# Gate, up and MLP-up products: from one 512-wide and one 256-wide product per weight block to three 256-wide ones, with the activations at the shifted place

## The chip, the cores and the metric

The kernel runs on one core of one Trainium2 chip. The metric is the device time of one execution in microseconds (us). TensorE (PE) multiplies into PSUM, VectorE (DVE) and ScalarE (ACT) read PSUM and SBUF, GpSimd (POOL) does a few small things, SyncE (SP) issues the weight transfers.

## The reference

Two model blocks run one after the other on 256 tokens of width 1024, all in float32. The first block has two layers (a multiscale pooling mixer, then a differential attention), each followed by a layernorm and a SwiGLU feed-forward part (FFN) of width 2816 with its own layernorm. The second block has a token mixer with many projections, and an MLP of width 4096 with a squared relu:

```python
def _swiglu(x, w_gate, w_up, w_down):
    return (jax.nn.silu(x @ w_gate) * (x @ w_up)) @ w_down

for i in range(DEPTH):                       # 2 layers
    h = pool or attention (x)
    x = _layernorm(ALPHA * x + h, ln_mix_g[i], ln_mix_b[i])
    x = _layernorm(ALPHA * x + _swiglu(x, w_gate[i], w_up[i], w_down[i]), ln_ffn_g[i], ln_ffn_b[i])

x = x + token_mixer(rms_norm(x, norm_mix_g), w_in, ...)
x = x + jnp.square(jax.nn.relu(rms_norm(x, norm_mlp_g) @ w_up)) @ w_down
return rms_norm(x, final_norm_g)
```

The change touches `x @ w_gate`, `x @ w_up` of the two FFNs and `x @ w_up` of the MLP.

## The kernel before, in words

**Precision in three products.** Every float32 operand of a large product is split into a rounded part and its remainder (`w_hi` and `w_lo` for weights, `x_hi` and `x_lo` for activations, type fp32r), and a product is the sum w_hi·x_hi + w_hi·x_lo + w_lo·x_hi in PSUM.

**Units.** Weights stream through three slots. A unit is 1 MB of weights, 2048 numbers in each of the 128 partitions. SP loads it into `raw` by two transfers of 512 KB (each waits until `lo_done` says that the slot is free), ACT rounds it into `w_hi` (two instructions, L1043), DVE takes the remainder into `w_lo` (two instructions, L1055, signalled by `lo_done`), and PE uses it (`unit_done` counts the units that PE has finished). A gate or up unit holds 1024 rows by 256 columns of weights: eight blocks k of 128 rows, two blocks j of 128 columns. All matrix products are recorded at line L505 (`mm`), so the operand names tell them apart: `bank<-x_both,w_hi` has weights stationary and activations moving, `bank<-w_hi,arena_r` is the down product, with the hidden values stationary and the down weights moving, 512 columns at a time.

**Gate and up before.** `apart` uses that x_hi and x_lo lie beside each other in `x_both`: for a block (j, k) one product of w_hi with 512 moving columns gives both halves, and one of w_lo with the 256 columns of x_hi adds to the first half. The two column blocks j of a unit take two whole PSUM banks (gate 4 and 5, up 6 and 7), and DVE adds the halves afterwards (`both_halves`, a tensor_reduce at L1515). `project_apart` runs all w_hi products of a unit and then all w_lo products, or the other way round (`narrow_first`, for up). A unit is thus 16 products of 512 and 16 of 256 columns.

**Three products elsewhere.** The attention heads and the projections of the token mixer use `project`, which makes for each block three products of 256 columns into half a bank (`three`): w_hi·x_hi, w_hi·x_lo, w_lo·x_hi. The last up of each FFN and of the MLP uses it too (`final=True`), so DVE adds nothing there.

**Two places for x_both.** `x_cells` has 48 spare numbers. `x_both` starts at its beginning (the near place), `x_far` 48 numbers (192 bytes) later (the far place: `far_hi`, `far_lo`). `normed` says where a norm writes: far for the norms ahead of the attention (V_NORM) and ahead of the token mixer (MIX_NORM), near for the norms ahead of both FFNs and of the MLP. The final ups mentioned above thus run `project` on the near place, the heads and the mixer on the far one.

**An FFN chunk.** The FFN goes through 11 chunks of 256 hidden columns (`NCH`), each a gate unit, an up unit and the down unit of the chunk before. PE waits with a gate for `gate_read` (DVE has read banks 4 and 5 of the chunk before) and with an up for `up_read`. DVE's order in a chunk is: remainder of one unit, `gate_total` (adds the gate's halves), remainder of the next unit, `silu`, `hidden` (adds the up's halves and multiplies), remainder, `low`. ACT takes the tanh of the added gate from SBUF (L1105) and rounds the hidden values (L1112). The MLP (`pe_mlp`, `v_mlp`, `s_mlp`) has 16 chunks of an up and a down unit; there DVE adds the halves and squares.

**The first units of a stage.** `first_apart` starts on the first four k as soon as their activations are ready. In the first FFN the order on DVE is: remainders of units 0, 1 and 2 (six instructions), `gate_total(0)`, remainder of unit 3, `silu(0)`, `hidden(0)`. Unit 3 (the second up) can be loaded only when unit 0's slot is free. The third unit on PE is the gate of chunk 1.

## Time and profile before

| | |
|---|---|
| median of 3 runs | 964.71 us (963.29 to 966.46) |
| the profiled execution | 966.28 us, of which 964.5 us are its span |
| PE busy | 951.7 us, 99% of the span, 5903 matmuls |
| PE weight loads (beside the matmuls) | 840.5 us, 87% |
| DVE busy | 674.4 us, 70% |
| ACT busy | 468.5 us, 49% |
| TensorE clock granted, mean | 0.997 |

A matmul's duration in the records (some 280 ns for 256 columns, 390 ns for 512) contains the way through the array and overlaps with the next one. What a stream of matmuls costs is the distance from one start to the next, read from the timeline: start of a row to the start of a later one, divided by the number of matmuls between. In the timeline each row is: start in us, length in us, engine, line, operation, result and operands, shape, number of instructions merged, and in brackets the idle time before it and what ended it. A few matmul records are missing from the trace, so counts are taken from the code where the timeline shows fewer.

### The profile page before, as it was taken

Reading aid. Unit: us, or ns where it says so; the run is one execution under the profiler, and the core shown is the slowest. Engines: PE = TensorE matmul, PEld = TensorE weight load, DVE = VectorE, ACT = ScalarE, POOL = GpSimd, SP = SyncE. Lnnn points to the kernel's source line nnn. Section 1 sums busy time; section 2 is a strip of 40 time slices with the busy share of each in tenths; the row PEclk is TensorE's granted clock in tenths of the full one; section 3 lists DMA queues with packets and bytes.
Section 4 is the critical chain, followed back from the end, with each engine's and each line's share of the span. In section 5 each row is a group of like instructions: output and inputs, shape, how many; then the busy total and the mean of one; then the engine's idle time right before and its main releaser. Section 6 shows DMA issues by size and latency. Waiting matters only on the chain.

```text
span 964.5 us, 15378 instructions
## 1 busy us (share of the span) xinstructions
PE 951.7 (99%) x5903; PEld 840.5 (87%) x5903; DVE 674.4 (70%) x968; ACT 468.5 (49%) x721; POOL 34.6 (4%) x63
## 2 busy tenths in 40 slices
PE   9999999999999999999999999999999999999997
PEld 8888888887898888888898989899999888888886
DVE  2877676776687886767768577886876676666663
ACT  3454344335766443434435556566654453443432
POOL 2100001000000100000001000000000000000000
PEclk9999999999999999999999999999999999999999
DMA  8666666548632566565653855445566546565541
GB/s 296 203 214 220 204 207 238 187 174 226 168 132 89 170 221 206 202 206 175 214 175 125 238 157 144 138 132 154 175 209 201 182 137 211 185 206 178 202 145 43
DMA packets 142160, 175.67 MB, mean 182 GB/s; under 512 B 7152, under 2 KB 121009, under 8 KB 142110
## 3 DMA queue, kind: packets, MB, share of 16 engines
q1 hardware_dynamic: 138896, 166.55, 53.9%
q0 software_dynamic: 2656, 8.31, 2.6%
q8 instruction: 34, 0.56, 0.2%
q10 hardware_dynamic: 558, 0.12, 0.1%
q14 instruction: 16, 0.13, 0.0%
HBM read 173.88 MB, written 1.09 MB: 181 GB/s over the span
## 4 chain that ended last, share of the span: by engine, by line
PE 93%; DVE 4%; ACT 2%; issue 1%; POOL 0%; DVEq 0%; POOLq 0%
PE bank L505 91%; PE bank L752 1%; DVE x_both L1443 1%; PE bank L629 1%; DVE w_lo L1055 0%; DVE x_rows L1471 0%; DVE x_rows L1464 0%; DVE stats L1456 0%; ACT w_hi L1043 0%; ACT x_both L1082 0%; ACT arena L1331 0%; PE bank L641 0%; ACT arena L1168 0%; DVE arena L1645 0%; ACT arena L1307 0%
## 5 line engine op out<-in xcount | busy, mean ns | idle before, releaser
L505 PE MATMUL bank<-x_both,w_hi 128*128 128x256 f32 (+1 forms) x2112 | 428.1, 328 | 0.5 <-DVE x_both L1443 0.5
L1055 DVE TENSOR_TENSOR w_lo<-raw,w_hi 128x1024 fp32r<-128x1024 f32 x308 | 362.6, 1221 | 92.3 <-ACT w_hi L1043 92.1
L505 PEld LDWEIGHTS bank<-x_both,w_hi 128*128 128x128 f32 x2112 | 351.5, 188 | 40.9 <-issue 6.5
L1043 ACT ACTIVATE w_hi<-raw 128x1024 fp32r<-128x1024 f32 x308 | 308.0, 1049 | 99.3 <-PE bank L505 95.0
L505 PE MATMUL bank<-x_both,w_lo 128*128 128x256 f32 (+1 forms) x1512 | 282.6, 281 | 0.0
L505 PEld LDWEIGHTS bank<-x_both,w_lo 128*128 128x128 f32 (+1 forms) x1512 | 227.3, 190 | 3.0
L505 PE MATMUL bank<-w_hi,arena_r 128*128 128x512 f32 x672 | 189.6, 391 | 0.2 <-DVE arena_r L1592 0.2
L505 PEld LDWEIGHTS bank<-w_hi,arena_r 128*128 128x128 f32 x672 | 124.8, 188 | 25.7 <-issue 0.8
L505 PE MATMUL bank<-w_lo,arena_r 128*128 128x512 f32 x336 | 106.3, 390 | 0.0
L1515 DVE TENSOR_REDUCE arena<-bank 128x512 f32<-128x1024 f32 x57 | 69.7, 1223 | 47.9 <-PE bank L505 47.9
L505 PEld LDWEIGHTS bank<-w_lo,arena_r 128*128 128x128 f32 x336 | 63.1, 188 | 13.2
L1105 ACT ACTIVATE arena<-arena 128x512 f32<-128x512 f32 x22 | 13.9, 632 | 92.9 <-DVE arena L1515 92.9
L505 PE MATMUL bank<-arena 128*128 128x128 f32 (+5 forms) x368 | 54.3, 350 | 3.2 <-ACT arena L1203 2.1
L505 PE MATMUL bank<-w_hi,x_both 128*128 128x512 f32 x192 | 55.9, 395 | 1.0 <-DVE x_both L1443 1.0
L505 PEld LDWEIGHTS bank<-arena 64*128 64x128 f32 (+2 forms) x368 | 38.4, 190 | 13.3 <-issue 6.8
L1112 ACT ACTIVATE arena_r<-arena 128x512 fp32r<-128x512 f32 x22 | 13.9, 634 | 70.1 <-PE bank L505 60.5
L505 PEld LDWEIGHTS bank<-w_hi,x_both 128*128 128x128 f32 x192 | 35.8, 188 | 10.1 <-issue 1.8
L1203 ACT ACTIVATE arena<-bank 128x512 f32<-128x512 f32 x22 | 13.1, 597 | 49.8 <-PE bank L505 49.8
L1548 DVE TENSOR_TENSOR arena_r<-arena,arena_r 128x512 fp32r<-128x512 f32 x22 | 15.2, 692 | 31.4 <-ACT arena_r L1112 31.4
L1139 ACT ACTIVATE arena_r<-arena 128x512 fp32r<-128x512 f32 x16 | 10.1, 634 | 55.1 <-PE bank L505 48.1
L505 PE MATMUL bank<-arena_r,w_hi 128*128 128x256 f32 x192 | 32.9, 276 | 0.0
L505 PE MATMUL bank<-w_lo,x_both 128*128 128x512 f32 x96 | 31.9, 392 | 0.0
(168 smaller groups left out, 600.9 us busy)
## 6 DMA issues: line engine op xcount, KB each, us to landing
raw<-w_up SPq DMA_DIRECT2D x76, 512.0 KB, 4.5
raw<-w_down SPq DMA_DIRECT2D x76, 512.0 KB, 4.1
raw<-w_in SPq DMA_DIRECT2D x60, 512.0 KB, 4.6
raw<-w_gate SPq DMA_DIRECT2D x44, 512.0 KB, 4.7
raw<-w_qkv SPq DMA_DIRECT2D x24, 512.0 KB, 4.8
raw<-w_o SPq DMA_DIRECT2D x16, 512.0 KB, 4.0
table<-bias_vectors POOLq DMA_DIRECT2D x12, 256.0 KB, 4.2
raw<-w_pa SPq DMA_DIRECT2D x4, 512.0 KB, 4.4
```

Of the source, the lines that this page charges most:

```text
L505: return nc.tensor.matmul(*a, skip_group_check=True, **k)
L629: last = nc.tensor.transpose(b[:, k * P:(k + 1) * P], src[:, i, (4 * h + k) * P:(4 * h + k + 1) * P], ident[:, :])
L752: last = nc.tensor.transpose(bank[6 + m][:, c], prob[:, m, c], ident[:, :])
L1043: nc.scalar.activation(w_hi[slot][:, c], raw[slot][:, c], ACT.Copy).then_inc(hi_done, 1)
L1055: last = nc.vector.tensor_tensor(w_lo[slot][:, c], raw[slot][:, c], w_hi[slot][:, c].bitcast(F32), ALU.subtract)
L1105: nc.scalar.activation(ffn_e.rearrange("p (a b) -> p a b", a=2), gate_sum, ACT.Tanh, scale=0.5).then_inc(tanh_done, 1)
L1112: nc.scalar.activation(h_hi[buf], hidden_rows, ACT.Copy).then_inc(h_rounded, 1)
L1139: nc.scalar.activation(h_hi[buf], hidden_rows, ACT.Copy).then_inc(m_rounded, 1)
L1203: nc.scalar.activation(dst, both, ACT.Copy).then_inc(proj_copied, 1)
L1443: V.tensor_tensor(lo[:, k, q], src, hi[:, k, q].bitcast(F32), ALU.subtract).then_inc(x_ready, 1)
L1515: return V.tensor_reduce(o, banks8[:, b:b + 2, :].rearrange("p a (h t) -> p a t h", h=2), mybir.AxisListType.X, ALU.add)
L1548: V.tensor_tensor(h_lo[buf], ffn_h.rearrange("p (a b) -> p a b", a=2), h_hi[buf].bitcast(F32), ALU.subtract).then_inc(h_ready, 1)
```

## The change

The two FFNs and the MLP use `project` for all gates and ups, so each unit is 48 products of 256 columns instead of 16 of 512 and 16 of 256. A new `first_project` does the same for the first units: per half of k all w_hi products, first x_hi and then x_lo, and at the end the w_lo products. A unit's result is one bank (gate 4, up 6; MLP 4, its second chunk 6). `both_halves` and its semaphores go. `tanh_of` and the relu (now on ACT for all chunks) read the bank itself; `silu`, `hidden` and `square` on DVE take one operand from the bank. `gate_read`, for which PE waits with the next gate, is now signalled by `silu`, and PE waits with the next up for `product_done` in place of `up_read`. All norms write x_both at the far place.

```diff
-        def apart(banks, w, cols, ks, first):
-            for j, b in enumerate(banks):
-                for k in ks:
-                    last = mm(b[:, 0:cols], w[:, k, j * P:(j + 1) * P], x_both[:, k, 0:cols],
-                              start=(first and k == 0), stop=(not first and k == KT - 1))
-            return last
...
-        def first_apart(eng, unit, rounds, banks):
+        def first_project(eng, unit, rounds, outs):
             whi, wlo = (part(w, unit % SLOTS, KT) for w in (w_hi, w_lo))
             eng.wait_ge(hi_done, 2 * unit + 2)
             for h in range(2):
                 eng.wait_ge(x_ready, 4 * rounds + 2 * h + 2)
-                apart(banks, whi, 2 * SEQ, range(4 * h, 4 * h + 4), True)
+                for j, o in enumerate(outs):
+                    for k in range(4 * h, 4 * h + 4):
+                        for src in (far_hi, far_lo):
+                            mm(o, whi[:, k, j * P:(j + 1) * P], src[:, k, :],
+                               start=(j == 0 and k == 0 and src is far_hi), stop=False)
             eng.wait_ge(lo_done, unit + 1)
-            return apart(banks, wlo, SEQ, range(KT), False)
+            for j, o in enumerate(outs):
+                for k in range(KT):
+                    last = mm(o, wlo[:, k, j * P:(j + 1) * P], far_hi[:, k, :], start=False, stop=(k == KT - 1))
+            return last
...
         def normed(ev):
-            return (far_hi, far_lo) if ev in (V_NORM, MIX_NORM) else (x_hi, x_lo)
+            return far_hi, far_lo
...
-            def gate_up(i, unit, final=False):
+            def gate_up(i, unit):
                 eng.wait_ge(lo_done, unit + 1)
                 eng.wait_ge(gate_read, i + f * NCH)
-                project_apart(slots[0], pair45).then_inc(unit_done, 1)
+                project(slots[0], two4, far_hi, far_lo).then_inc(unit_done, 1)
                 eng.wait_ge(lo_done, unit + 2)
-                eng.wait_ge(up_read, i + f * NCH)
-                if final:
-                    project(slots[1], two6, x_hi, x_lo).then_inc(unit_done, 1)
-                else:
-                    project_apart(slots[1], pair67, True).then_inc(unit_done, 1)
+                eng.wait_ge(product_done, i + f * NCH)
+                project(slots[1], two6, far_hi, far_lo).then_inc(unit_done, 1)
...
-            first_apart(eng, u0, rounds, pair45).then_inc(unit_done, 1)
-            eng.wait_ge(hi_done, 2 * u0 + 4)
-            project_apart((u0 + 1) % SLOTS, pair67, False,
-                          lambda: eng.wait_ge(lo_done, u0 + 2)).then_inc(unit_done, 1)
+            first_project(eng, u0, rounds, two4).then_inc(unit_done, 1)
+            first_project(eng, u0 + 1, rounds, two6).then_inc(unit_done, 1)
             gate_up(1, u0 + 2)
...
         def s_ffn(eng, f):
-            def tanh_of(i):
-                eng.wait_ge(gate_read, i + (f * NCH + 1))
-                nc.scalar.activation(ffn_e.rearrange("p (a b) -> p a b", a=2), gate_sum, ACT.Tanh,
-                                     scale=0.5).then_inc(tanh_done, 1)
+            def tanh_of(i, gate_unit, begin=False):
+                eng.wait_ge(unit_done, gate_unit + 1)
+                if not begin:
+                    eng.wait_ge(gate_read, i + f * NCH)
+                nc.scalar.activation(ffn_e, bank[4][:, :], ACT.Tanh, scale=0.5).then_inc(tanh_done, 1)
...
+            def relu(i, unit, b=4, begin=False):
+                eng.wait_ge(unit_done, unit + 1)
+                if not begin:
+                    eng.wait_ge(sq_done, i)
+                nc.scalar.activation(ffn_e, bank[b][:, :], ACT.Relu).then_inc(relu_done, 1)
...
-        def both_halves(o, b):
-            return V.tensor_reduce(o, banks8[:, b:b + 2, :].rearrange("p a (h t) -> p a t h", h=2),
-                                   mybir.AxisListType.X, ALU.add)
...
             def silu(i):
                 eng.wait_ge(tanh_done, i + (f * NCH + 1))
-                V.scalar_tensor_tensor(ffn_t, ffn_e, 1.0, gate_sum.rearrange("p a b -> p (a b)"), ALU.add,
-                                       ALU.mult).then_inc(silu_done, 1)
+                V.scalar_tensor_tensor(ffn_t, ffn_e, 1.0, bank[4][:, :], ALU.add, ALU.mult).then_inc(gate_read, 1)
...
             v_split(eng, u0 + 2)
-            gate_total(0, u0)
             v_split(eng, u0 + 3)
             silu(0)
             hidden(0, u0 + 1)
```

PE at the start of an FFN, from its first product to the gate of chunk 1, before (the wait for `gate_read` is that of the third unit):

```order
L505 MATMUL bank<-x_both,w_hi 128x512 [waits x_ready,hi_done]
L505 MATMUL bank<-x_both,w_hi 128x512 x7
L505 MATMUL bank<-x_both,w_hi 128x512 [waits x_ready]
L505 MATMUL bank<-x_both,w_hi 128x512 x7
L505 MATMUL bank<-x_both,w_lo 128x256 [waits lo_done]
L505 MATMUL bank<-x_both,w_lo 128x256 x15
L505 MATMUL bank<-x_both,w_hi 128x512 [waits hi_done]
L505 MATMUL bank<-x_both,w_hi 128x512 x15
L505 MATMUL bank<-x_both,w_lo 128x256 [waits lo_done]
L505 MATMUL bank<-x_both,w_lo 128x256 x15
L505 MATMUL bank<-x_both,w_hi 128x512 [waits gate_read,lo_done]
L505 MATMUL bank<-x_both,w_hi 128x512 x15
```

and now, from the second unit on (mm is now at L501):

```order
L501 MATMUL bank<-x_both,w_hi 128x256 [waits x_ready,hi_done]
L501 MATMUL bank<-x_both,w_hi 128x256 x15
L501 MATMUL bank<-x_both,w_hi 128x256 [waits x_ready]
L501 MATMUL bank<-x_both,w_hi 128x256 x15
L501 MATMUL bank<-x_both,w_lo 128x256 [waits lo_done]
L501 MATMUL bank<-x_both,w_lo 128x256 x15
L501 MATMUL bank<-x_both,w_hi 128x256 [waits gate_read,lo_done]
L501 MATMUL bank<-x_both,w_hi 128x256
L501 MATMUL bank<-x_both,w_lo 128x256
L501 MATMUL bank<-x_both,w_hi 128x256 x2
```

The 512-wide products became pairs of 256-wide ones; the gate of chunk 1 still waits for `gate_read`. DVE at the same place, before (the first row holds the remainders of units 0, 1 and 2, L1515 adds the halves and signals `gate_read` at its first row here):

```order
L1055 TENSOR_TENSOR w_lo<-raw,w_hi 128x1024 [waits hi_done] x6
L1515 TENSOR_REDUCE arena<-bank 128x512 [waits unit_done]
L1055 TENSOR_TENSOR w_lo<-raw,w_hi 128x1024 [waits hi_done] x2
L1529 SCALAR_TENSOR_TENSOR arena<-arena 128x512 [waits tanh_done]
L1515 TENSOR_REDUCE arena<-bank 128x512 [waits unit_done]
L1540 SCALAR_TENSOR_TENSOR arena<-arena 128x512 [waits silu_done,up_read]
L1548 TENSOR_TENSOR arena_r<-arena,arena_r 128x512 [waits h_rounded]
```

and now (L1507 is `silu`, which signals `gate_read`; L1512 is `hidden`):

```order
L1030 TENSOR_TENSOR w_lo<-raw,w_hi 128x1024 [waits hi_done] x8
L1507 SCALAR_TENSOR_TENSOR arena<-arena,bank 128x512 [waits tanh_done]
L1512 SCALAR_TENSOR_TENSOR arena<-arena,bank 128x512 [waits gate_read,unit_done]
L1516 TENSOR_TENSOR arena_r<-arena,arena_r 128x512 [waits h_rounded]
L1524 UNCONDITIONAL_BRANCH
```

`gate_read` moved from an instruction that stood ahead of the remainder of unit 3 to one that stands behind it.

## Rows read from the trace of the kernel before

**Rows 1.** The page: busy time of each engine, and the shares of the chain.
```profile
PE 951.7 (99%) x5903; PEld 840.5 (87%) x5903; DVE 674.4 (70%) x968; ACT 468.5 (49%) x721; POOL 34.6 (4%) x63
PE 93%; DVE 4%; ACT 2%; issue 1%; POOL 0%; DVEq 0%; POOLq 0%
```
**Rows 2.** Timeline of PE: one chunk of the first FFN.
```profile
60.21 3.79 PE L505 MATMUL bank<-x_both,w_hi 128*128 128x512 f32 x16
63.84 4.00 PE L505 MATMUL bank<-x_both,w_lo 128*128 128x256 f32 x32
67.67 3.82 PE L505 MATMUL bank<-x_both,w_hi 128*128 128x512 f32 x16
71.32 0.62 PE L505 MATMUL bank<-w_hi,arena_r 128*128 128x512 f32 x2
...
76.76 3.79 PE L505 MATMUL bank<-x_both,w_hi 128*128 128x512 f32 x16
```
**Rows 3.** Timeline of PE: one chunk of the MLP.
```profile
919.52 3.79 PE L505 MATMUL bank<-x_both,w_hi 128*128 128x512 f32 x16
923.15 2.08 PE L505 MATMUL bank<-x_both,w_lo 128*128 128x256 f32 x16
925.06 0.63 PE L505 MATMUL bank<-w_hi,arena_r 128*128 128x512 f32 x2
...
930.53 3.79 PE L505 MATMUL bank<-x_both,w_hi 128*128 128x512 f32 x16
```
**Rows 4.** Timeline of PE: token mixer's gates, 32 triples at the far place.
```profile
705.99 0.39 PE L505 MATMUL bank<-x_both,w_hi 128*128 128x256 f32 x2
...
716.53 0.39 PE L505 MATMUL bank<-x_both,w_hi 128*128 128x256 f32 x2
```
**Rows 5.** Timeline of PE: first projections of the mixer, 40 triples, far place.
```profile
534.12 0.40 PE L505 MATMUL bank<-x_both,w_hi 128*128 128x256 f32 x2
...
547.90 0.40 PE L505 MATMUL bank<-x_both,w_hi 128*72 128x256 f32 x2
```
**Rows 6.** Timeline of PE: the MLP's last up, 16 triples, near place.
```profile
941.53 0.40 PE L505 MATMUL bank<-x_both,w_hi 128*128 128x256 f32 x2
...
946.93 0.40 PE L505 MATMUL bank<-x_both,w_hi 128*128 128x256 f32 x2
```
**Rows 7.** Timeline of PE: start of the first FFN.
```profile
32.40 3.91 PE L505 MATMUL bank<-x_both,w_hi 128*128 128x512 f32 x16 [0.17 <-DVE x_both L1443]
...
38.06 3.82 PE L505 MATMUL bank<-x_both,w_hi 128*128 128x512 f32 x16
...
43.63 3.82 PE L505 MATMUL bank<-x_both,w_hi 128*128 128x512 f32 x16
```
**Rows 8.** Timeline of SP's queue: the issue of unit 3.
```profile
35.75 0.92 SPq L391 DMA_DIRECT2D raw<-w_up  x2
```
**Rows 9.** Timeline of ACT: start of the first FFN.
```profile
41.43 0.63 ACT L1105 ACTIVATE arena<-arena 128x512 f32<-128x512 f32 x1 [5.44 <-DVE arena L1515]
42.68 2.01 ACT L1043 ACTIVATE w_hi<-raw 128x1024 fp32r<-128x1024 f32 x2 [0.62 <-DMA raw<-w_up]
```
**Rows 10.** Timeline of DVE: start of the first FFN.
```profile
40.17 1.22 DVE L1515 TENSOR_REDUCE arena<-bank 128x512 f32<-128x1024 f32 x1
43.77 2.36 DVE L1055 TENSOR_TENSOR w_lo<-raw,w_hi 128x1024 fp32r<-128x1024 f32 x2 [2.38 <-ACT w_hi L1043]
46.05 0.68 DVE L1529 SCALAR_TENSOR_TENSOR arena<-arena 128x512 f32<-128x512 f32 x1
```
**Rows 11.** Timeline of DVE: a loop chunk, and the start of the second FFN.
```profile
82.50 1.23 DVE L1515 TENSOR_REDUCE arena<-bank 128x512 f32<-128x1024 f32 x1 [1.56 <-PE bank L505]
...
87.65 0.69 DVE L1529 SCALAR_TENSOR_TENSOR arena<-arena 128x512 f32<-128x512 f32 x1
...
340.28 1.23 DVE L1515 TENSOR_REDUCE arena<-bank 128x512 f32<-128x1024 f32 x1 [0.26 <-PE bank L505]
```
**Rows 12.** One line of the kernel: the reduce that the change removes.
```profile
L1515 DVE TENSOR_REDUCE arena<-bank x57: 1217/1224/1227, 40.2 to 936.3; 128x512 f32<-128x1024 f32 x57
```
**Rows 13.** Stretches: PE, PEld, DVE, ACT, POOL busy, granted clock, DMA share.
```profile
7.00:10.40 3.40, 3.40 (x15) 1.79 (x15) 0.97 (x2) 0.35 (x1) 0.18 (x1) 1.00 0.88 270
10.50:13.80 3.30, 3.30 (x17) 3.30 (x16) 2.76 (x3) 1.79 (x4) 0.00 (x0) 0.50 1.09 379
```

More of the change, by code:

```diff
@@ L1139, in round_h @@
                 nc.scalar.activation(h_hi[buf], hidden_rows, ACT.Copy).then_inc(m_rounded, 1)
+            def relu(i, unit, b=4, begin=False):
+                eng.wait_ge(unit_done, unit + 1)
+                if not begin:
+                    eng.wait_ge(sq_done, i)
+                nc.scalar.activation(ffn_e, bank[b][:, :], ACT.Relu).then_inc(relu_done, 1)
             s_split(eng, U_MLP + 2)
+            relu(0, U_MLP, begin=True)
             round_h(0, None)
-            with eng.Fori(0, (NCH2 - 1) // 3 - 1) as i:
+            for j in range(3):
+                unit = U_MLP + 1 + 2 * j
+                s_split(eng, unit + 2)
+                relu(j + 1, unit, 4 if j else 6)
+                s_split(eng, unit + 3)
+                round_h(j + 1, unit + 2)
+            with eng.Fori(1, (NCH2 - 1) // 3 - 1) as i:
                 for j in range(3):
@@ L1152, in s_mlp @@
                 s_split(eng, unit + 2)
-                if c == NCH2 - 1:
-                    eng.wait_ge(unit_done, unit + 1)
-                    nc.scalar.activation(ffn_e, bank[4][:, :], ACT.Relu).then_inc(relu_done, 1)
+                relu(c, unit)
                 s_split(eng, unit + 3)
@@ L1568, in v_ffn @@
             v_split(eng, unit + 2)
-            gate_total(NCH - 1, unit)
             v_split(eng, unit + 3)
             silu(NCH - 1)
-            hidden(NCH - 1, unit + 1, bank[6][:, :])
+            hidden(NCH - 1, unit + 1)
             low(NCH - 1, 1)
@@ L1595, in v_mlp @@
             v_split(eng, U_MLP + 2)
[L1596 removed]
+            square(0, True)
             low(0)
@@ L1600, in v_mlp @@
                 v_split(eng, unit + 2)
-                square(j + 1, unit, b=4 if j else 6)
+                square(j + 1, b=4 if j else 6)
                 v_split(eng, unit + 3)
```

75 lines of the change are left out of this document (18 added, 57 removed).

## The prediction

> **What bounds the kernel now.** I read the page first: PE is busy for 951.7 of 964.5 us, and 93% of the chain that ended last is PE [rows 1]. So only two things count: how far apart matmuls start, and where PE is made to wait. Next the timeline of PE, since a matmul's recorded length says nothing of the distance to the next. In a chunk of the first FFN [rows 2] the 16 wide products of the gate take 63.84 - 60.21 = 3.63 us, 227 ns each; the 32 narrow ones of gate and up 3.83 us, 120 ns each; the wide ones of up 3.65 us; the 24 of the down product 5.44 us. The chunk's period is 16.55 us, without a gap. A chunk of the MLP takes 11.01 us, of which the down product, entered straight from narrow products, is 5.47 [rows 3]. DVE is 70% busy and waits for PE, so that it loses 57 reduces of 1.22 us [rows 12], 70 us of work, gives nothing by itself.
>
> **What three narrow products cost.** A block needs the same 768 columns either way. The trace shows three prices for a triple of 256-column products:
> - at the near place 0.360 us (15 distances in 5.40 us [rows 6]), 120 ns each;
> - at the far place in the mixer's gates 0.340 us (31 distances in 10.54 us [rows 4]), 113.3 ns each;
> - at the far place in the mixer's first projections 0.353 us (39 distances in 13.78 us [rows 5]), 117.8 ns each.
>
> The block before costs 227 + 120 = 347 ns. So the same edit is a gain of 7 ns a block at the fast far pace, a loss of 6 at the slow far pace and of 13 at the near pace; a unit has 16 blocks. The far place alone does not make the pace fast: going through the timeline by triples, far streams keep one pace from their first few matmuls to their end, over unit boundaries too. Of 22 entries into such a stream between 240.77 and 656.81 us, 12 settle at the fast pace and 10 at the slow one; most of them follow small matmuls and a pause of the array.
>
> Which pace will the FFN have? Its gates are entered straight from 24 evenly spaced wide products of the down unit, with no pause. Evenly spaced wide products run at 113.3 ns per 256 columns, just the fast pace, so nothing has to settle; that speaks for it. The one far stream that follows wide products directly without small ones between, and is slow [rows 5], speaks against. I take the fast pace for the chunks, and half and half for the units entered after small matmuls or a pause.
>
> **The sum at the fast pace.**
> - A chunk of an FFN in the loop: 32 triples at 0.340 are 10.88 us, and the down product, now entered from narrow ones, 5.47 [rows 3]: 16.35 against 16.55, -0.20. There are nine per layer, 18: -3.6 us.
> - The last chunk of each layer: gate 5.55 to 5.44, and the last up, which ran at the near place, 5.76 to 5.44: -0.43, twice: -0.86. The MLP's last up likewise: -0.32.
> - 14 further MLP chunks: 5.44 + 5.47 = 10.91 against 11.01: -1.4.
> - The first two units of the second FFN and the first of the MLP: -0.3.
> Together -6.5 us.
>
> **The new wait.** The gate of chunk 1 writes bank 4, which `silu(0)` now reads, so it waits for `silu(0)`. In the first FFN that instruction stands behind the remainder of unit 3. SP issues unit 3 at 35.75 [rows 8], when unit 0's slot is free. ACT waits for the transfer and starts to round at 42.68; this wait of 0.62 us is ended by the DMA, and before it ACT did the tanh [rows 9]. DVE takes the remainder from 43.77 and starts `silu(0)` at 46.05 [rows 10]. The tanh will be earlier, since it needs no reduce, but it is not what comes last: the transfer is, and its issue hangs on unit 0's remainder, which doesn't move. With 0.68 for `silu` (one operand in PSUM instead of SBUF, which I take at the same price; the far bound is the 1.22 of the reduce) and 0.1 for the signal, PE starts that gate at 46.83 instead of 43.63 [rows 7]: +3.2 us. What the first two units gain or lose there is hidden in this wait and counts nothing. Queued behind the waiting matmul is everything on PE; nothing there was idle before, so the 3.2 us stay.
>
> Elsewhere the wait has cover. In a loop chunk the gate ends at 82.50 and `silu` starts at 87.65 [rows 11], earlier once the reduce is gone, while the next gate starts at 76.76 + 16.55 = 93.3 [rows 2]. The next up waits for `hidden`, which needs the up before and 0.7 us, against 11 us of other work. In the second FFN the first gate's end shows at 340.28 [rows 11]; tanh 0.6, the first half of rounding 1.05, two remainders 2.4 and `silu` 0.7 make 344.9 to 345.1, and PE wants the gate of chunk 1 at 334.43 + 11.0 = 345.4. That is a cover of 0.3 to 0.5 us; were the tanh or the transfer late by 1 us, it would cost 0.5. In the MLP relu and square (1.3 us) lie beside a down product of 5.4.
>
> **Units entered after a pause.** Chunk 1 of the first FFN (after the new wait), four units of the second FFN and the first two of the MLP are entered like the mixer's units. At the slow pace each costs 16 x 13.3 ns = 0.21 us more; eight units at half chance: +0.85.
>
> Sum: -6.5 + 3.2 + 0.85 = -2.5 us. The profiled execution took 966.28 us, its span 964.5 and 1.8 around it; the change would make it 963.8. The median shown lies 1.6 us below that execution, so the forecast for the median is 964.71 - 2.5 = 962.2 us.
>
> **What might add to it.** A pause can cost clock. Early in the trace PE ran at full clock on matmuls with a single row of weights, and in the stretch after it, 10.50 to 13.80, it was granted 0.50, 1.2 GHz instead of 2.4 [rows 13]. If the new wait has the same effect, 3.3 us at half the clock lose 1.65 us: 963.9. I leave that inside the likeliest case, as its upper part.
>
> **Rivals.**
> 1. *The slow far pace in the chunks.* 32 triples at 0.353 plus 5.47 are 16.78, +0.23 a chunk, 18 times 4.1; an MLP chunk 11.12, +0.11, 14 times 1.6; the first units +0.3, the last ones about 0 (+0.11 and -0.11 per layer, -0.11 in the MLP). With the wait: 5.9 + 3.2 = +9.1, 973.8 us. For it: 10 of 22 entries, and [rows 5]. It decides from a pace of some 116 ns per product, where the gain of the chunks is gone and the wait remains: slower.
> 2. *Chunks of both paces,* half each: (-6.5 + 5.9) / 2 + 3.2 = +2.9, 967.6 us. For it: the heads and mixer units change pace from one entry to the next. Against: all chunks have one and the same entry.
> 3. *A fixed cost per matmul,* so that 256 columns cost 120 wherever they read. Then a chunk takes 11.52 + 5.47 = 16.99, +0.44, 18 times 7.9; last chunks +0.4, the MLP 14 x 0.22 = 3.1, first units 0.6; with the wait +15.2, 979.9 us. For it: near narrow and wide products both lie 13 ns above 256 and 512 columns at 2.4 GHz. Against: [rows 4] run at 113.3 over units on end.
> 4. *The wait does not come,* because the second up's transfer lands earlier or its order gives way: -6.5 + 0.4 = 958.6 us. The waiting order is in the code and the landing in [rows 9], so little speaks for it.
>
> The Trainium skill ("TensorE: Matmul & The Clock Gate", Back-to-back issue gap) states a warm distance of N / 2.4 + 2.5 ns, a fixed cost for each matmul. By it a block would go from 325 to 328 ns, some 2.3 us over 57 units, and with the wait the time would be about 970. Its direction is that of rival 3. The rows disagree with its size: they show 227 where it gives 216, and 113 or 120 where it gives 109.
>
> **How the numbers follow.** Chances: the forecast 0.57 (with and without loss of clock, 960.5 to 964.5), rival 1 0.20, rival 2 0.12, rival 3 0.04, rival 4 0.05, anything else 0.02. A measurement of this kernel tells 0.3% (2.9 us) from no change, so faster means below 961.8 and slower above 967.6. The forecast lies just inside no change: I give 0.23 of its 0.57 to faster and 0.34 to the same; rival 2 lies across the upper bound. Faster: 0.23 + 0.05 + 0.02 = 0.30. Same: 0.34 + 0.03 = 0.37. Slower: 0.20 + 0.09 + 0.04 = 0.33. The range has to take in rival 2 and most of rival 1: 960.0 to 974.0; the forecast's own is 960.5 to 964.5.
>
> **What the changed kernel's profile would show.** The step on the wait: PE idle some 3.3 us before the third unit of the first FFN, ended by the DVE instruction of `silu`, which starts near 46.05; nothing of the kind in the second FFN. The step on the pace: an FFN chunk of 16.35 us and triples 0.340 us apart; 16.78 and 0.353 mean rival 1, 16.99 and 0.360 rival 3. The loss of clock: a stretch at 0.50 behind the wait. DVE busy falls by some 70 us, and that should show in nothing else. I am wrong if the chunks' pace is not the fast one, or if PE doesn't wait for `silu(0)`.

## The result, and the profile after

The changed kernel took 974.96 us (median of 4 runs, 973.04 to 980.05) beside 965.59 us for the kernel before: a ratio of 1.0108, 95% interval [1.0076, 1.014]. It is slower by 1.1%. The forecast was 962.2 us, with a range of 960.0 to 974.0. The pace of the chunks is that of the first rival, priced at 973.8 us; how near that sum lies is in part luck, as the part on the prediction shows.

The profiled execution took 973.04 us with a span of 971.2; before it was 964.5. The page after, its busy times and the chain [rows 1]:

```profile
PE 954.8 (98%) x6815; PEld 879.8 (91%) x6815; DVE 609.5 (63%) x911; ACT 475.1 (49%) x736; POOL 34.6 (4%) x63
PE 91%; DVE 5%; ACT 2%; issue 1%; DMA 1%; POOL 0%; DVEq 0%; POOLq 0%; SPq 0%
```

The removed reduces took 69.7 us [rows 12]; DVE's busy time fell by 64.9 us, which shows nowhere in the time. The timeline of PE at the starts of two successive chunks of the first FFN, and of two of the MLP [rows 2, 3]:

```profile
63.22 0.40 PE L501 MATMUL bank<-x_both,w_hi 128*128 128x256 f32 x2
...
74.53 0.61 PE L501 MATMUL bank<-w_hi,arena_r 128*128 128x512 f32 x2
...
79.97 0.40 PE L501 MATMUL bank<-x_both,w_hi 128*128 128x256 f32 x2
...
804.20 0.40 PE L501 MATMUL bank<-x_both,w_hi 128*128 128x256 f32 x2
...
815.29 0.40 PE L501 MATMUL bank<-x_both,w_hi 128*128 128x256 f32 x2
```

A chunk takes 79.97 - 63.22 = 16.75 us where it took 16.55, and the 96 narrow products of gate and up end at 74.53: 11.31 us, 117.8 ns each. A chunk of the MLP takes 11.09 instead of 11.01. Every stream behind a down unit has this pace, in both FFNs and in the MLP. The new wait, in the timelines of PE, DVE and ACT [rows 7, 9, 10]:

```profile
29.99 1.18 PE L501 MATMUL bank<-x_both,w_hi 128*128 128x256 f32 x8 [0.17 <-DVE x_both L1431]
...
45.16 0.47 PE L501 MATMUL bank<-x_both,w_hi 128*128 128x256 f32 x2 [3.62 <-DVE arena L1507]
```
```profile
42.05 2.36 DVE L1030 TENSOR_TENSOR w_lo<-raw,w_hi 128x1024 fp32r<-128x1024 f32 x2 [4.20 <-ACT w_hi L1018]
44.33 0.68 DVE L1507 SCALAR_TENSOR_TENSOR arena<-arena,bank 128x512 f32<-128x512 f32 x1
```
```profile
35.92 0.60 ACT L1082 ACTIVATE arena<-bank 128x512 f32<-128x512 f32 x1 [2.35 <-PE bank L501]
40.96 2.00 ACT L1018 ACTIVATE w_hi<-raw 128x1024 fp32r<-128x1024 f32 x2 [4.44 <-DMA raw<-w_up]
```

PE stood still for 3.62 us before the gate of chunk 1, until `silu(0)` (L1507) was done at 45.01. The tanh was ready at 36.5; what came last was the transfer of unit 3, as the prediction's step said. What the pause did to the clock, in stretches (PE, PEld, DVE, ACT, POOL busy, granted clock, DMA share, GB/s) [rows 13]:

```profile
43.40:46.70 3.30, 1.54 (x12) 1.57 (x13) 2.50 (x4) 2.47 (x6) 0.00 (x0) 0.96 0.65 173
46.80:50.00 3.20, 3.20 (x18) 3.20 (x17) 2.75 (x3) 1.56 (x2) 0.00 (x0) 0.52 0.73 259
50.10:53.30 3.20, 3.20 (x31) 3.20 (x30) 0.00 (x0) 0.77 (x2) 0.00 (x0) 1.00 0.72 229
```

Behind the pause PE was granted 0.52, in the main 1.2 GHz instead of 2.4, for some 3.2 us, and was at full clock before and after. Chunk 1 took 63.22 - 45.16 = 18.06 us, 1.31 more than the chunk behind it. That is the net of two things: the last 70 narrow products or so of chunk 1 ran at 113.3 ns where those of the next chunk ran at 117.8, which saves 0.3 us, so that the clock by itself cost some 1.6 us (an estimate from these distances).

Stage by stage, distances between the same first matmuls in the two timelines, before and after: start of the first FFN to the gate of chunk 1, 11.23 and 15.17 (+3.94); chunk 1, 16.58 and 18.06 (+1.48); from there to the first head, 180.56 and 182.06 (+1.50); heads 93.66 and 93.67; second FFN 199.69 and 201.56 (+1.87); mixer 247.66 and 247.26 (-0.40); MLP 176.68 and 177.41 (+0.73). These make +9.12 us. The first FFN itself began 2.41 us earlier, at 29.99 instead of 32.40, which leaves the 6.7 us between the two spans; the medians differ by 9.4. No instruction ahead of it changed. What goes with the later start is a loss of clock in the opening. The stretch that [rows 13] shows at 0.50 is here at full clock:

```profile
10.50:13.80 3.30, 3.30 (x31) 3.30 (x30) 2.45 (x2) 2.62 (x6) 0.00 (x0) 1.00 1.09 382
```

Of the 19 profiled executions of this document five were granted 0.50 to 0.58 in that stretch (the kernel before, e3, e6, e7, e9); these begin the first FFN at 32.1 to 32.5 us, and the other 14, granted 1.00 there, between 29.3 and 30.4. It falls on kernels without regard to their edits, so spans are compared from the first FFN on.

### The profile page after: what moved, and what is told of

It reads as the page before. It is cut to its first block, busy times and chain, and to the rows that moved or that the text cites. A ratio compares the mean times of both kernels' runs of the same rounds, so it can differ in the third digit from the quotient of the medians.

```text
span 971.2 us, 17195 instructions
## 1 busy us (share of the span) xinstructions
PE 954.8 (98%) x6815; PEld 879.8 (91%) x6815; DVE 609.5 (63%) x911; ACT 475.1 (49%) x736; POOL 34.6 (4%) x63
## 4 chain that ended last, share of the span: by engine, by line
PE 91%; DVE 5%; ACT 2%; issue 1%; DMA 1%; POOL 0%; DVEq 0%; POOLq 0%; SPq 0%
PE bank L501 90%; PE bank L727 1%; DVE w_lo L1030 1%; DMA raw<-w_up 1%; DVE x_both L1431 1%; PE bank L612 0%; DVE x_rows L1459 0%; DVE x_rows L1452 0%; ACT w_hi L1018 0%; DVE stats L1444 0%; ACT x_both L1057 0%; ACT arena L1319 0%; PE bank L624 0%; ACT arena L1156 0%; DVE arena L1602 0%
## 5 line engine op out<-in xcount | busy, mean ns | idle before, releaser
L501 PE MATMUL bank<-x_both,w_hi 128*128 128x256 f32 (+1 forms) x3024 | 526.6, 281 | 4.1 <-DVE arena L1507 3.6
L501 PEld LDWEIGHTS bank<-x_both,w_hi 128*128 128x128 f32 (+1 forms) x3024 | 457.7, 188 | 13.0 <-issue 6.5
L501 PE MATMUL bank<-x_both,w_lo 128*128 128x256 f32 (+1 forms) x1512 | 411.1, 280 | 0.0
L501 PEld LDWEIGHTS bank<-x_both,w_lo 128*128 128x128 f32 (+1 forms) x1512 | 282.7, 191 | 0.0
L501 PE MATMUL bank<-w_hi,arena_r 128*128 128x512 f32 x672 | 189.2, 390 | 0.2 <-DVE arena_r L1549 0.2
L501 PEld LDWEIGHTS bank<-w_hi,arena_r 128*128 128x128 f32 x672 | 123.4, 188 | 24.0 <-issue 0.8
L501 PE MATMUL bank<-w_lo,arena_r 128*128 128x512 f32 x336 | 106.1, 389 | 0.0
L501 PEld LDWEIGHTS bank<-w_lo,arena_r 128*128 128x128 f32 x336 | 63.1, 188 | 13.1
L501 PE MATMUL bank<-w_hi,x_both 128*128 128x512 f32 x192 | 56.0, 396 | 1.0 <-DVE x_both L1431 1.0
L501 PE MATMUL bank<-arena 128*128 128x128 f32 (+5 forms) x368 | 53.4, 346 | 3.2 <-ACT arena L1191 2.1
L501 PEld LDWEIGHTS bank<-arena 64*128 64x128 f32 (+2 forms) x368 | 37.6, 186 | 13.3 <-issue 6.8
L1088 ACT ACTIVATE arena_r<-arena 128x512 fp32r<-128x512 f32 x22 | 13.9, 631 | 72.2 <-PE bank L501 61.8
L1082 ACT ACTIVATE arena<-bank 128x512 f32<-128x512 f32 x22 | 13.2, 599 | 70.1 <-PE bank L501 70.1
L501 PEld LDWEIGHTS bank<-w_hi,x_both 128*128 128x128 f32 x192 | 35.7, 188 | 10.1 <-issue 1.8
L1191 ACT ACTIVATE arena<-bank 128x512 f32<-128x512 f32 x22 | 13.1, 597 | 49.4 <-PE bank L501 49.4
L1121 ACT ACTIVATE arena<-bank 128x512 f32<-128x512 f32 x16 | 9.6, 599 | 49.7 <-PE bank L501 49.7
L501 PE MATMUL bank<-arena_r,w_hi 128*128 128x256 f32 x192 | 32.9, 276 | 0.0
L1545 DVE SCALAR_TENSOR_TENSOR arena<-bank,arena 128x512 f32<-128x512 f32 x16 | 11.1, 692 | 34.5 <-ACT arena L1121 34.5
L501 PE MATMUL bank<-w_lo,x_both 128*128 128x512 f32 x96 | 31.8, 391 | 0.0
```

The source lines that it names most:

```text
L501: return nc.tensor.matmul(*a, skip_group_check=True, **k)
L1082: nc.scalar.activation(ffn_e, bank[4][:, :], ACT.Tanh, scale=0.5).then_inc(tanh_done, 1)
L1088: nc.scalar.activation(h_hi[buf], hidden_rows, ACT.Copy).then_inc(h_rounded, 1)
L1121: nc.scalar.activation(ffn_e, bank[b][:, :], ACT.Relu).then_inc(relu_done, 1)
L1191: nc.scalar.activation(dst, both, ACT.Copy).then_inc(proj_copied, 1)
L1545: V.scalar_tensor_tensor(ffn_h, bank[b][:, :], 0.0, ffn_e, ALU.max, ALU.mult).then_inc(sq_done, 1)
```

## The experiments

Two things had to be told apart: the wait with its clock, about 5.4 us, and the pace of the streams, the rest. The disputed question is why products that read the same x at the same far place run at 117.8 ns in one stream and at 113.3 in another.

One thing varies under all of them. The 864 products of the mixer's gates run at 113.3 ns in the kernels before and after, in e1, e7, e9, e10 and e11, and at 117.8 in e2, e3, e5 and e6, though nothing there was edited and x lies at 192 bytes in each: 3.9 us. A time of one run therefore says less than the chunks in its trace, whose lengths repeat to 0.01 us within an execution.

**e1: silu(0) ahead of the remainder of unit 3** (in the changed kernel).
```diff
             v_split(eng, u0 + 2)
-            v_split(eng, u0 + 3)
             silu(0)
+            v_split(eng, u0 + 3)
             hidden(0, u0 + 1)
```


> The changed kernel with silu(0) placed ahead of the remainder of unit 3 on DVE, so that in the first FFN the gate of chunk 1 no longer waits for the transfer. Theory A (the wait is a cost of its own, and it alone takes the clock): PE idle before that gate falls from 3.62 us to none, the stretch behind it is granted 1.00 instead of 0.52, chunk 1 takes 16.75 instead of 18.06 us, together about 5 us less than the changed kernel; chunks stay at 16.75. Rival: something else on PE or DVE waits in its place (the next up for the product, the down for its weights), and less than 2 us come back.

Measured: 970.36 us (10 runs), ratio to before 1.0036 [1.002, 1.0053], against 1.0108 for the change. The medians differ by 4.6 us, the ratios by 0.7%, and from the start of the first FFN to the end the two traces differ by 6.0 us. (The execution in e1's trace, 966.71 us, was the fastest of the ten; what the other nine lost, 2.6 to 5.3 us, no trace shows.) The wait and the stretch at half clock are gone; in e2, which keeps the wait, PE stood still for 3.85 us and was again granted 0.50 from 46.6 to 50.0. The first units of both FFNs, entered behind transposes, ran at 113.3 this time. The chunks did not move; two starts in the timeline of PE:
```profile
73.69 0.40 PE L501 MATMUL bank<-x_both,w_hi 128*128 128x256 f32 x2
...
90.44 0.40 PE L501 MATMUL bank<-x_both,w_hi 128*128 128x256 f32 x2
```
So 16.75 us belongs to the chunk and not to the wait, and a loss of 0.36% remains with it.

**Places: e2 (near), e4 (64 bytes), e12 (128 bytes), e8 (384 bytes).** All four are the changed kernel with x elsewhere; e4, e8 and e12 have `silu(0)` early. In e2 the heads and the mixer stay at 192 bytes, in the other three they move along.
```diff
 # e2: gate, up and MLP-up (and their norms) use x_hi, x_lo for far_hi, far_lo
-project(slots[0], two4, far_hi, far_lo)
+project(slots[0], two4, x_hi, x_lo)
 # e4, e12, e8: x_far starts XS = 16, 32, 96 floats behind x_both (SHIFT is 48)
-        x_both, x_far = (... for at in (0, SHIFT))
+        x_both, x_far = (... for at in (0, XS))
```


> The changed kernel with the FFN and MLP activations back at the near place, three 256-wide products kept (the mixer and the heads stay far). Theory A (the place sets the pace, 120 ns per product near, 113.3 or 117.8 far): FFN chunks of 17.0 us, MLP chunks of 11.2 us, some 6 us above the changed kernel. Rival (the place has no part in it, the slow pace comes from what runs before): chunks stay at 16.75 and 11.09 us, the time at that of the changed kernel.

> The changed kernel with silu(0) early, and the far place 64 bytes behind the near one instead of 192 (the arenas stay where they are). If the pace hangs on the distance of moving data and weights in the address, narrow products get another pace than 117.8 in all chunks alike: 113.3 (chunk 16.35 us) or 120 (17.0 us). Rival (it hangs on the entry from the wide products alone): 117.8 and 16.75 us as with 192 bytes.

> The kernel of e1 with x_both 128 bytes behind the near place (0 and 384 bytes gave 120.0 behind a down unit; 64 gave 117.8 everywhere; 192 gives 117.8 behind a down unit and 113.3 in part of the others). Theory 'period of 128 bytes': 120.0, chunk 16.98 to 17.0 us, about 983 us. Theory 'period of 384 bytes or more': between, 117.8 or 113.3, chunk 16.75 to 16.79 us or 16.32.

> The kernel of e1 with x_both 384 bytes behind the near place instead of 192. In e2 (0 bytes) the streams ran at 120.0, in e4 (64 bytes) at 117.8 everywhere, in e1 (192 bytes) at 113.3 or 117.8. Theory 'period' (the pace depends on the place modulo a small number of bytes, 128 or 64 or so): 384 is 0 modulo 128 and would run like the near place, 120.0, chunk 16.98 us. Theory 'distance' (only a place near to the weights' alignment is bad): 113.3 or 117.8 as in e1, or all 113.3.

Single runs: 984.09, 975.94, 982.49 and 982.68 us. Near, at 128 and at 384 bytes the chunk's streams run at 120.0 in the mean; at 64 bytes all of them, and the mixer's 864 products, at 117.8. Starts of two successive chunks in e12, and in e4, and in e4 one stream of the mixer:
```profile
75.58 0.40 PE L503 MATMUL bank<-x_both,w_hi 128*128 128x256 f32 x2
...
92.58 0.40 PE L503 MATMUL bank<-x_both,w_hi 128*128 128x256 f32 x2
```
```profile
74.82 0.40 PE L503 MATMUL bank<-x_both,w_hi 128*128 128x256 f32 x2
...
91.61 0.40 PE L503 MATMUL bank<-x_both,w_hi 128*128 128x256 f32 x2
...
627.67 0.28 PE L503 MATMUL bank<-x_both,w_lo 128*128 128x256 f32 x1
...
632.43 0.28 PE L503 MATMUL bank<-x_both,w_lo 128*128 128x256 f32 x1
```
The chunks take 17.00 and 16.79 us. In the chunks the place repeats in its mean: 0, 128 and 384 bytes give 120.0. They are not the same rhythm, though. The three distances of a triple are 120, 120, 120 ns in e2 but 122, 118, 120 in e12 and 123, 117, 120 in e8, and outside of the chunks, in the first units of the FFNs, in the heads and in the mixer, most streams of e12 and e8 run at 118.5 to 118.8. Nor is the fast rhythm bound to 192 bytes: at 64 bytes the mixer's stream shown takes 4.76 us for 14 triples, 113.3 ns a product, the only one of e4 that does. So 64 and 192 bytes both have 113.3 and 117.8, and differ in how often they fall into each; why stays open.

**e3: the kernel before with everything at the far place.**
```diff
-mm(b[:, 0:cols], w[:, k, j * P:(j + 1) * P], x_both[:, k, 0:cols],
+mm(b[:, 0:cols], w[:, k, j * P:(j + 1) * P], x_far[:, k, 0:cols],
```


> The kernel before with only the place changed: all norms write far, the 512-wide and 256-wide products read far, DVE still adds the halves. Theory A (narrow products collide with their weight loads by place; wide ones leave the load time to spare): narrow ones at 113.3 or 117.8 ns instead of 120, wide ones at 227: chunks of 16.34 to 16.48 us instead of 16.55, 1 to 5 us faster than before. Rival (wide products lose at the far place as the rows of the mixer seem to, 229 to 236 ns at their start): chunks of 16.6 us or more, slower than before.

Measured: 966.99 us (10 runs), ratio 0.9991 [0.9967, 1.0015]. One chunk:
```profile
60.19 3.89 PE L505 MATMUL bank<-x_both,w_hi 128*128 128x512 f32 x16
63.92 3.80 PE L505 MATMUL bank<-x_both,w_lo 128*128 128x256 f32 x32
67.56 3.89 PE L505 MATMUL bank<-x_both,w_hi 128*128 128x512 f32 x16
...
76.75 3.89 PE L505 MATMUL bank<-x_both,w_hi 128*128 128x512 f32 x16
```
The narrow products fell from 120 to 114 ns and the wide ones rose from 227 to 233: 16.56 us as before. The far place is good for one form and bad for the other.

**e5: one product of 128 columns ahead of each gate from chunk 1 on and of each MLP-up that follows a down unit; e10: the same with 32 columns** (both on e1).
```diff
                 eng.wait_ge(gate_read, i + f * NCH)
+                mm(bank[5][:, 0:P], x_far[:, 0, 0:P], x_far[:, 0, 0:P], start=True, stop=True)
                 project(slots[0], two4, far_hi, far_lo)
```


> The kernel of e1 with one more TensorE product of 128 columns, into a bank that nobody reads, ahead of every gate unit and every MLP up that follows a down unit (17 + 22 of them, some 0.06 to 0.13 us each, 2 to 5 us in all if nothing else changes). In e1 each of these streams begins at 117 to 118 ns between products and stays at 117.8; only the streams that follow narrow transposes in the same kernel (29.64, 332.73) settle at 113.3. Theory 'entry' (a stream keeps whichever of two rhythms its first few products fall into, and the wide down products hand over the slow one): the gate streams begin with another gap and part or all of them run at 113.3; a chunk of 16.75 us becomes 16.32 plus the extra product. Theory 'neighbour' (the slow rhythm belongs to streams whose chunk holds wide products, whatever stands directly ahead): all stay at 117.8 and the run is 2 to 5 us longer than e1.

> The kernel of e5 with 32 columns instead of 128 in the added product. Theory 'entry': what matters is that the stream's first product begins early against its weight load; 32 columns do it as well, the streams run at 113.3 and the chunk is 16.40 to 16.47 us; ratio to before 0.996 to 0.999. If the number of columns decides which rhythm is met, the streams stay at 117.8 and the chunk is 16.75 to 16.85 us (ratio 1.003 to 1.006).

Measured: e5 964.77 us (one run), e10 964.17 us (12 runs), ratio 0.9992 [0.9978, 1.0006]. It is 34 such products in the code and the trace, not 39: 32 streams behind a down unit, and the gate of chunk 1 in each FFN, which stands behind narrow products. All 32 ran at 113.3 in both kernels. The gate of chunk 1 in e5's second FFN went from 113.3 to 117.8 across the added product, and in the first FFN from 117.8 to 113.3. Two entries of e5:
```profile
73.67 0.22 PE L501 MATMUL bank<-x_both 128*128 128x128 f32 x1
...
90.14 0.22 PE L501 MATMUL bank<-x_both 128*128 128x128 f32 x1
```
With one more product in it, the chunk fell from 16.75 to 16.47 us. Whether a load is longer is seen in the groups of PE's weight loads (name, shapes, count, busy us, mean ns), first in e1 from 74 to 84 us (pace 117.8), then in e5 from 75 to 84 (113.3):
```profile
L501 PEld LDWEIGHTS bank<-x_both,w_hi 128*128 128x128 f32 x58 | 8.8, 188 | 0.0
L501 PEld LDWEIGHTS bank<-x_both,w_lo 128*128 128x128 f32 x29 | 5.6, 192 | 0.0
```
```profile
L501 PEld LDWEIGHTS bank<-x_both,w_hi 128*128 128x128 f32 x54 | 8.2, 188 | 0.0
L501 PEld LDWEIGHTS bank<-x_both,w_lo 128*128 128x128 f32 x27 | 5.1, 188 | 0.0
```
In the slow rhythm of e1 it is the load of w_lo alone that is longer, one in three; in e2, at 120.0, all three show 192. It does not hold as a rule: e4 and e15 have 117.8 with loads of 187 and 188 ns, and e12 and e8 have 120.0 with 189 for all. So the longer loads are not shown to be the cause of a pace.

**e6: a product of 512 columns ahead; e7: the products of a triple in another order.**
```diff
+                mm(bank[5][:, :], x_far[:, 0, 0:P], x_far[:, 0, :], start=True, stop=True)   # e6
 # e7, for each k: wlo x hi, whi x hi, whi x lo   (was: whi x hi, whi x lo, wlo x hi)
```


> The same as e5 with a product of 512 columns (moving: x at the far place) instead of one of 128, 39 of them at 0.227 us, 9 us in all. In e3 the narrow streams that follow wide products over x at the far place begin at 121 or 122, 116, 114 and settle at 113.3. Theory 'entry': if what matters is the last moving operand ahead of the stream (x far rather than the down weights), these streams settle at 113.3: chunk 16.32 + 0.23 = 16.55 us. If it is the form of the stream (in e3 one x operand for every product, here two in turn), they stay at 117.8: chunk 16.98 us.

> The kernel of e1 with the three products of a tile in another order (weight rest times x high, then weight times x high, weight times x low) in gate, up and MLP up that follow the first two units. Same reads, same count. Theory 'entry': the first product's stationary operand is in another buffer and the first gaps differ, so the streams after a down unit may settle at 113.3 (chunk 16.32 us, MLP chunk 10.88). Theory 'place' (the pace follows from where the operands lie): 117.8 throughout, chunk 16.75 us, MLP 11.09, the time of e1 (970) within 0.3%.

Single runs: 981.02 and 969.08 us. All 32 streams behind a down unit (e6: behind the wide product that follows it) stayed at 117.8. The two gates of chunk 1 in e6, where the wide product stands between narrow ones at 113.3, stayed at 113.3. So one wide product only adds its own time (a chunk takes 17.00 us) and leaves the rhythm as it is, and the order of the three is no matter.

**e9: no product more, the first one in two halves.**
```diff
+                    if in_two and (j, k) == (0, 0):
+                        mm(o[:, 0:P], whi[:, k, c], hi[:, k, 0:P], start=True, stop=False)
+                        mm(o[:, P:SEQ], whi[:, k, c], hi[:, k, P:SEQ], start=False, stop=False)
```


> The kernel of e1 with the first product of each gate unit and of each MLP up (the one right behind the down unit) issued as two products of 128 columns; no column more or less in all. In e5 one more product of 128 columns ahead of these streams took them from 117.8 to 113.3 ns, at a cost of 58 + 59 ns and a few slower gaps behind it (chunk 16.47 where 144 such gaps less would give 16.32). Theory 'entry' (a narrow product between the wide ones and the stream shifts its rhythm): these streams settle at 113.3 with at most 0.06 us paid at each entry, chunk 16.38 to 16.42 us, MLP chunk 10.94 to 10.98; 17 x 0.08 + 22 x 0.08 = 3 us below e5's, about 0.4% below the kernel before. Rival: the added product helped only since it was one operation more or came from another bank, and the streams stay at 117.8: chunk 16.75 to 16.81 us, ratio to before 1.003 to 1.005.

Measured: 963.28 us (12 runs), ratio 0.9986 [0.9968, 1.0004]. All at 113.3:
```profile
76.03 0.50 PE L501 MATMUL bank<-x_both,w_hi 128*128 128x128 f32 x3
...
92.49 0.50 PE L501 MATMUL bank<-x_both,w_hi 128*128 128x128 f32 x3
```
16.46 us, not the 16.38 to 16.42 expected: an entry costs 0.12 us, half of it in the two halves (169 ns for 113) and half in the first full product behind them (172 ns). The MLP's chunk is 11.01 us, just what it was before the change.

**e11: x near again, with the small product ahead; e15: x near, and w_hi and w_lo 192 bytes further; e14: the kernel before, with w_lo alone 192 bytes further.**
```diff
+        sb("ahead_w_lo", [P, 48], F32R)
         w_lo = [sb(f"w_lo{s}", [P, UW], F32R) for s in range(SLOTS)]
+        sb("behind_w_lo", [P, 80], F32R)
```


> The kernel of e2 (gate, up and MLP up read x at the near place) with silu(0) early as in e1 and the added product of e5 ahead of gate and MLP up. Theory 'place and entry' (the near place has one pace, 120.0, whatever stands ahead; only the far place has two): 120.0 stays, chunk 16.98 + 0.1 to 0.15 us, about 983 us. Theory 'entry alone': the streams run at 113.3 at the near place too, chunk 16.47 us, about 966 us.

> The kernel of e2 with silu(0) early, and w_hi and w_lo both 192 bytes further while x is read at the near place in gate, up and MLP up. Theory 'relative place': these streams run at 117.8 (or 113.3) as in e1 and not at 120.0, chunk 16.75 us (16.32). Theory 'place of x alone': 120.0, chunk 16.98 us. The mixer and the heads, which read x 192 bytes further, would by 'relative place' now meet the 120.0.

> The kernel before with one edit: the buffers of the weights' rests (w_lo) lie 192 bytes further, x stays at the near place for gate, up and MLP-up, the wide products (227 ns) untouched. Theory 'relative place' (the pace of a product depends on where its moving operand lies against the stationary operand loaded in the meantime): the narrow products w_lo times x_hi, 120.0 at the same place, run at 113.3 or 117.8, the wide ones stay at 227; FFN chunk 16.55 - 32 x 6.7 = 16.34 us (or 16.48), MLP chunk 11.01 - 0.11 = 10.90; ratio to before 0.993 to 0.996 (0.998 at 117.8). Theory 'place of x alone': nothing changes, 120.0, ratio 1.000.

e11, one run, 979.53 us: 120.0 in all these streams. The entry chooses between two rhythms at the far place; near, no stream showed a second one. e15, one run, 983.18 us: near x now runs at 117.8 behind down units and at 113.3 in the first units of both FFNs, and the mixer, whose x and weights both lie 192 bytes further, at 120.0, where it never was in another kernel with x at 192 bytes. A chunk (16.91 us, with a slower down unit in it), and a triple of the mixer's gates (0.36 us):
```profile
74.63 0.40 PE L505 MATMUL bank<-x_both,w_hi 128*128 128x256 f32 x2
...
91.54 0.40 PE L505 MATMUL bank<-x_both,w_hi 128*128 128x256 f32 x2
...
705.84 0.40 PE L505 MATMUL bank<-x_both,w_hi 128*128 128x256 f32 x2
706.08 0.28 PE L505 MATMUL bank<-x_both,w_lo 128*128 128x256 f32 x1
706.20 0.40 PE L505 MATMUL bank<-x_both,w_hi 128*128 128x256 f32 x2
```
So in these streams the place counts as a distance between the operand that streams and the one that is loaded. e14 (5 runs) took 974.01 us, ratio 1.0111 [1.0093, 1.0129]. The direction held for the narrow products, 117.8, but the gain I expected was lost: the down unit streams the weights past h, and the distance of w_lo had changed too: it rose to 232 ns a product (233 in e15, where both w_hi and w_lo moved). In the MLP:
```profile
921.08 0.64 PE L507 MATMUL bank<-w_hi,arena_r 128*128 128x512 f32 x2
...
926.65 3.80 PE L507 MATMUL bank<-x_both,w_hi 128*128 128x512 f32 x16
```
The down unit takes 5.57 us where it took 5.47 [rows 3]. Together the FFN's chunks (16.62 us for 16.55) and the MLP's (11.09 for 11.01) lose 2.4 us. The mixer's 864 products ran at 117.8 too (+3.9 us), but they do so in e3 as well, where no weight was moved.

**e13 and e17: the split entry at the heads, the mixer's projections and its first gate too; e16: the same outside of the chunks in the kernel before.**
```diff
-                    last = project(s, proj_out(unit), far_hi, far_lo)
+                    last = project(s, proj_out(unit), far_hi, far_lo, in_two=True)
```


> The kernel of e9 with the first product in two halves also at the head projections, the mixer's projections (among them the 120 products that run at 117.8 behind wide ones in every kernel so far) and the first gate unit of the mixer (864 products, 113.3 in some kernels and 117.8 in others). Theory 'entry': the 120 settle at 113.3 (120 x 4.5 = 0.5 us), the head streams at 117.8 (some 7 of 16, 48 x 4.5 = 0.2 us each) too, and the 864 run at 113.3; each entry costs 0.06 us, 25 entries 1.5 us; in all 0 to 1.5 us less than e9, ratio to before 0.997 to 0.999. Rival: outside the chunks the pace follows something else (the heads' 256-column moving weights stand ahead, or what the other engines do), and the streams stay mixed.

> The kernel before with the first product in two halves at the head projections, the mixer's projections and its first gate unit, as in e13; its gate, up and MLP units in the form of before. Theory 'the change pays a little at the fast pace' (FFN chunk 16.46 against 16.55, 18 x 0.09 = 1.6 us, nothing in the MLP): this kernel keeps only the mixer's part of e13's gain, 1 to 2 us, ratio to before 0.998 to 1.000, and e13's kernel is 1 to 2 us faster. Rival 'the whole gain is the split entry in the mixer': the same time as e13's kernel beside it, ratio 0.997.

> The kernel of e13 again, beside e16. Theory 'the change pays a little at the fast pace': ratio to before 0.996 to 0.998 again, 1 to 2 us below e16. Rival: the same as e16 within 0.5 us. If its first gate units or the 864 products of the mixer fall to 117.8 in this execution, up to 2 us more.

The 120 products named in the expectation of e13 had not run at 117.8 in every kernel: in the changed kernel, in e2 and in e10 they ran at 113.3 but for their last part.

e13: 961.63 us, ratio 0.9973 [0.9962, 0.9984]. e17, the same kernel again: 961.41 us, 0.9973 [0.9959, 0.9987]. Beside it e16: 964.77 us, 1.0006 [0.9991, 1.0021]. So the split entry outside of the chunks wins nothing in the kernel before, and the changed form with `silu(0)` early and split entries is faster than both kernels, by 0.27%: 3.4 us below e16. The expectation of e16 gave 1 to 2 us of the gain to the mixer's part, which had none of it. What the form itself wins is 18 x 0.09 in the FFNs' loops and the 1.2 us that the prediction counted for the last chunks, whose ups had run at the near place: 2.8 of the 3.4. In the mixer the split entries hit the fast rhythm mostly (the gates' 864 products, 12 of 14 other streams and part of a 13th), at the heads only 3 times in 8 in e13 and 4 in e17.

## Why the prediction was wrong

**The step that failed** is "I take the fast pace for the chunks". Its reason was that evenly spaced wide products run at 113.3 ns per 256 columns, so that "nothing has to settle". The runs show the reverse: all 32 streams entered straight from a down unit ran at 117.8 in the changed kernel, in e1 and in e7, and a half-width product between takes all 32 to 113.3 (e5, e9, e10).

The evidence against was also misread. The prediction calls [rows 5] the one far stream that follows wide products directly. There were two in the trace before, and the other one, the first head's at 240.77, settled at the fast pace, 45 distances in 5.12 us:

```profile
240.31 0.62 PE L505 MATMUL bank<-w_hi,x_both 128*128 128x512 f32 x2
240.77 0.40 PE L505 MATMUL bank<-x_both,w_hi 128*128 128x256 f32 x2
...
245.89 0.39 PE L505 MATMUL bank<-x_both,w_hi 128*128 128x256 f32 x2
```

In the changed kernel the two had changed sides: the head's ran at 117.8, and that of [rows 5] at 113.3 from its sixth product until its 96th, where weights of 72 columns begin. The wide products ahead of both are uneven, 226, 229 and 232 ns in turn, where those of a down unit are all 227. So no row before had the entry of the chunks, and the rows that came nearest stood one to one. Nothing but the argument "nothing has to settle" set the fast pace at 0.57 against 0.20 for rival 1.

**That rival 1's sum came so near is luck.** Its pace was right: a chunk of 16.75 us (16.78 priced), and 11.09 in the MLP (11.12). But it had +5.9 us for pace and first units, which measured some +4.3 (0.20 and 0.08 a chunk, not 0.23 and 0.11), and +3.2 for the wait, which with its clock measured some 5.2; the mixer, whose 120 products of [rows 5] had become faster, gave 0.4 back. Two terms that are off in opposite directions brought the same +9.1 as the stages add up to.

**The wait** was right in its place, its releaser and its chain. The size was 3.94 us and not 3.2: from SP's issue of unit 3 to ACT's rounding it was 40.96 - 33.34 = 7.62 us, and 42.68 - 35.75 = 6.93 before [rows 8, 9]. The price of `silu` with an operand in PSUM, 0.68, was right. No wait came in the second FFN or the MLP.

**The clock** was left as the upper part of the forecast. It came: some 1.6 us by itself, 1.3 net of the faster products in the same chunk, and 1.65 predicted. At 0.52 of full clock the size agrees with [rows 13]. Those rows gave no cause, though: PE was busy all through the stretch ahead of that loss, and stood still for 3.62 us ahead of this one. e1 takes both away.

**Units after a pause.** Half and half was a fair guess: the first units ran slow, the MLP's fast; in e1 it was the other way round.

**The gain at the fast pace** was over-sized as well. 16.35 us a chunk counted no price for the entry; e9's 16.46 has 0.12 for it. So the MLP has nothing to win (11.01 both ways) and the FFNs 0.09 a chunk instead of 0.20.

**The removed reduces** changed nothing in the time, as said; DVE's busy time fell by 64.9 us, not by some 70.

**Rival 3 and the rule of the Trainium skill.** That a fixed cost per matmul sets the pace is excluded: the same 96 products cost 10.9, 11.3 and 11.5 us by place and entry alone. The time of 974.96 lies nearer to the 970 that the rule of the Trainium skill ("TensorE: Matmul & The Clock Gate", Back-to-back issue gap) gave than to my forecast, but by a wrong cause; the same section calls that formula the gap of an isolated matmul and not of a stream. The Trainium skill ("SBUF — State Buffer", SBUF: two separate sides) says that on the engines' side only the port pair shared by VectorE and GpSimd causes contention, and that TensorE never waits on anyone. Whatever TensorE does between its own two reads, e2, e14 and e15 show that their distance in memory shifts its pace by 2 to 7 ns a product; the cause inside the engine was not measured.

## What to carry to other kernels

Price a stream of matmuls from a row with the same operand places and the same instruction directly ahead of it, and when no row has that entry, give the paces seen elsewhere even chances: a row with a similar entry changed sides from one kernel to the next. Where streams of equal products run at two paces, try a half-width product at the entry before judging a change of form; here it decided between 1.0036 and 0.9986. It worked behind the evenly spaced wide products of the down unit, in 32 streams of 32; at the heads it did not, and behind narrow products one of them led into the slow rhythm. Moving one buffer changes its distance to every other operand it meets: price each product that reads it, as stationary and as moving.

## What was not expected of the hardware

- A stream of 256-column products ran at 113.3, 117.8, 118.7 or 120.0 ns a product in the mean. The distance of moving operand and weights sets which of them occur: 120.0 alone with x near, 118.7 or 120.0 at 128 and 384 bytes, 113.3 or 117.8 at 64 and 192. Within a pair the products ahead have a part in the choice. Once taken, a pace was mostly kept: 96 products in a chunk, 864 in the mixer. It changed after the stretch at half clock in the changed kernel, and where weights of 72 columns began.
- A wide product took 227 ns with x near and 233 at 192 bytes (e3), and in the down unit 227, or 231 to 233 with weights moved (e14, e15).
- A pause of 3.62 us was followed by some 3.2 us at 0.52 of full clock, and the stream that began behind it changed from 117.8 to 113.3 once the clock was back: the units before the pause ran at the one and most of chunk 1 at the other.
- Five of 19 profiled executions lost 3.4 us of full clock between 10 and 14 us and began the first FFN 1.7 to 3.1 us later than the others.
